# Two-block decoder forward pass: sums and splits at the start, the order of work in both attentions, and the heads and tails of the second block's layers

## The reference, cut to what matters

```python
# first block, two layers; adaptive scale, shift and gate come from silu(c) @ ada_w + ada_b
h  = rmsnorm(x,  norm_mix[i]) * (1.0 + sc1) + sh1
hc = rmsnorm(xc, norm_mix[i]) * (1.0 + csc1) + csh1
y, yc = diff_attention(...)  if i == 0 else neighbourhood_attention(...)   # q, k, v = h @ wqkv; o @ wo
x = x + g1 * y
x = x + g2 * conv_ffn(h2, ...)      # up, 3-tap conv, silu(g) * a, down; h2 = rmsnorm(x) scaled, shifted
# (xc is carried along the same way in layer 0)

# _diff_attend, layer 0: 8 heads, two maps each
p = softmax(s);  a = p[:, :, 0] - lam * p[:, :, 1];  o = rmsnorm(a @ v, subln) * (1.0 - lam_init)
# neighbourhood_attention, layer 1: 16 heads, scores + relative bias under a mask, then softmax @ v

# second block, two layers
h = rmsnorm_2(x, norm_g);  proj = h @ w_in          # nsa, pool, conv, fox, gates, merges
for i, o in enumerate((o_nsa, o_pool, o_conv, o_fox)):
    acc += sigmoid(merge[:, :, i]) * ((o * silu(gates[:, :, i])) @ w_branch[i])
x = x + acc @ w_out
# at the end
return rmsnorm_2(x, final_norm_g)
```

## Time and profile before

| | |
|---|---|
| median of 3 runs | 1707.87 us (1707.37 to 1710.95) |
| profiled execution | 1705.45 us, its span 1703.6 us, mean granted TensorE clock 0.983 |
| busy, share of the span | PE 1623.3 us (95%), PEld (weight loads, beside PE) 1421.4, DVE 874.5, ACT 743.6, POOL 540.6 |
| share of the chain that ended last | PE 87%, DVE 3%, POOL 3%, DMA 3%, issue 2%, ACT 2% |
| DMA | 249.39 MB, mean 146 GB/s |

### The profile page before, as it was taken

The page is one execution under the profiler, slowest core; times in us unless marked ns, Lnnn a source line. Parts: engine busy times, 40 slices in busy tenths (PEclk is TensorE's granted clock), DMA queues, the critical chain, the costliest instruction groups (busy, mean ns, idle before and its releaser), DMA issues.

```text
span 1703.6 us, 26688 instructions
## 1 busy us (share of the span) xinstructions
PE 1623.3 (95%) x10996; PEld 1421.4 (83%) x10996; DVE 874.5 (51%) x1382; ACT 743.6 (44%) x1341; POOL 540.6 (32%) x358
## 2 busy tenths in 40 slices
PE   8999986999999999999979999999999999999997
PEld 6679655868777888868957899999999999999997
DVE  3335375347533554333165688647475445468334
ACT  3323375345422443334256555445544444554342
POOL 1224045223210222220254111115423565433553
PEclk9999999999999999999999999999999999999998
DMA  9154401344246222366232455553535543534551
GB/s 393 51 222 173 177 22 50 102 170 173 84 167 230 79 81 84 118 211 215 94 75 83 145 184 180 155 189 128 194 125 173 174 167 120 198 124 134 185 181 46
DMA packets 52904, 249.39 MB, mean 146 GB/s; under 512 B 20656, under 2 KB 21680, under 8 KB 26288
## 3 DMA queue, kind: packets, MB, share of 16 engines
q1 hardware_dynamic: 44320, 244.42, 41.2%
q10 hardware_dynamic: 8464, 3.28, 0.8%
HBM read 246.63 MB, written 1.05 MB: 145 GB/s over the span
## 4 chain that ended last, share of the span: by engine, by line
PE 87%; DVE 3%; POOL 3%; DMA 3%; issue 2%; ACT 2%; POOLq 0%; DVEq 0%; SPq 0%; ACTq 0%
PE psq L520 19%; PE psq L521 19%; PE psq L522 19%; PE ps L520 6%; PE ps L522 6%; PE ps L521 6%; DMA RAW<-wstream 2%; PE ps L533 2%; PE ps L665 1%; PE psq L1022 1%; PE psq L1905 1%; DVE STAT L1074 1%; PE ps L579 1%; PE ps L1002 0%; DVE WL L502 0%
## 5 line engine op out<-in xcount | busy, mean ns | idle before, releaser
L520 PE MATMUL psq<-NH,WH 128*128 128x256 f32 (+1 forms) x1904 | 600.2, 315 | 13.6 <-POOL NL L2229 5.0
L521 PE MATMUL psq<-NL,WH 128*128 128x256 f32 (+1 forms) x1904 | 592.1, 311 | 0.0
L522 PE MATMUL psq<-NH,WL 128*128 128x256 f32 (+1 forms) x1904 | 592.0, 311 | 0.0
L502 DVE TENSOR_TENSOR WL<-RAW,WH 128x1024 fp32r<-128x1024 f32 (+3 forms) x264 | 322.9, 1247 | 387.2 <-ACT WH L492 387.2
L502 POOL TENSOR_TENSOR WL<-RAW,WH 128x1024 fp32r<-128x1024 f32 (+2 forms) x116 | 292.2, 2521 | 533.7 <-ACT WH L492 533.6
L492 ACT ACTIVATE WH<-RAW 128x1024 fp32r<-128x1024 f32 (+2 forms) x380 | 361.1, 1001 | 194.1 <-DMA RAW<-wstream 151.7
L520 PEld LDWEIGHTS psq<-NH,WH 128*128 128x128 f32 x1904 | 368.6, 194 | 45.9 <-issue 19.6
L522 PEld LDWEIGHTS psq<-NH,WL 128*128 128x128 f32 x1904 | 368.7, 194 | 18.2
L521 PEld LDWEIGHTS psq<-NL,WH 128*128 128x128 f32 x1904 | 369.2, 194 | 17.1
L520 PE MATMUL ps<-NH,WH 128*128 128x256 f32 (+1 forms) x368 | 121.9, 331 | 2.5 <-DVE WL L502 1.9
L521 PE MATMUL ps<-NL,WH 128*128 128x256 f32 (+1 forms) x368 | 121.2, 329 | 0.0
(11 more groups left out here) (326 smaller groups left out, 2543.7 us busy)
## 6 DMA issues: line engine op xcount, KB each, us to landing
RAW<-wstream SPq DMA_DIRECT2D x196, 1024.0 KB, 4.9
RAW<-wstream SPq DMA_DIRECT2D x32, 704.0 KB, 4.1
K<-first SPq DMA_DIRECT2D x4, 1024.0 KB, 13.1
X<-xin SPq DMA_DIRECT2D x2, 1024.0 KB, 6.0
V<-first SPq DMA_DIRECT2D x2, 1024.0 KB, 19.0
Q<-first SPq DMA_DIRECT2D x2, 1024.0 KB, 26.4
BR<-rpb ACTq DMA_DIRECT2D x8, 256.0 KB, 9.5
BR<-rpb SPq DMA_DIRECT2D x8, 256.0 KB, 8.5
```

Of the source, the lines that this page charges most:

```text
L502: e.tensor_tensor(WL[:, u % 3, a:z], RAW[:, v % 3, a:z], WH[:, u % 3, a:z].bitcast(F32), ALU.subtract).then_inc(w_lo_p if pool else w_lo_v, 1)
L520: e.matmul(o, lh, rh, start=start, stop=False)
L521: e.matmul(o, lh, rl, start=False, stop=False)
L522: return e.matmul(o, ll, rh, start=False, stop=stop)
```

## The change

The parts, in the order of the program:

1. Start: the square sums become eight matmuls with a block of ones 32 columns wide, in four strips of PSUM (`pe_strip_sums`), a copy and four one-column products (`pe_strip_join`). The constants are loaded in two parts, `first(0)` before unit 0, `first(1)` before unit 1, and so on. `FIRST_PIECES` is another table, and units 1 and 2 are split at j = 1, 2 instead of 1, 3.
2. Diff attention: `wo` units 0 to 2 are loaded before the `ada` 2 weights and split during the V projections; `ada` 2 runs in steps 2 to 9; DVE takes age 6 first in each step and then goes from young to old; the first four k of `wo` unit 0 run in steps 33 to 36, and head 7's turn stands before k = 6 and not k = 5.
3. Neighbourhood attention: scores of pairs 0 to 3 stand among the last V projection, whose four query tiles are now written one after the other (`pe_last_values`); bias chunk 3 is completed in steps 10 and 11; k = 0 to 5 of `wo` (1, 0) run in steps 17 to 20.
4. `wo` (1, 1) and (1, 2), `up` (1, 0) and `out` units 0 to 2 are multiplied k by k over both output tiles (`pe_tiles`, `pe_halves`), so that each k is wanted later than before; `wo` (1, 3) and `out` unit 3 finish in two products, one per output tile and bank.
5. Second block, both layers: `kc`, `qn`, `kn` are multiplied with x times the norm's gain, not yet divided by the root mean square; their high and low parts (`act_raw_hi`, `dve_raw_lo`) lie in the free half of `NH` and `NL` and are made as the residual tiles come; DVE multiplies by the row 1/rms when it copies the three results out (`dve_raw_out`, in place of ACT's copy). The usual norm runs beside these products. In layer 0, the residual x takes its own norm and gain after `kn`'s turn.
6. Last branch: the split of the next unit's `WL` stands behind the split of the sums.
7. End: the final gain is multiplied in by ACT when each tile is complete, then four DVE products of two tiles each, and four stores.

The diff, cut to its core:

```diff
+    for i in range(3):
+        add(("wo", 0, i), 1, run=False)
     for k in range(DT):
         add_ada(2, k)
         run_ada(2, k)
-    for i in range(4):
-        add(("wo", 0, i), 1000 if i else 1)
+    add(("wo", 0, 3), 1000, run=False)
+    runs += [("wo", 0, i) for i in range(4)]
...
-    on_pool = [[KEYS[v] == ("wo", 0, 0), v in SPLIT_AT and SPLIT_AT[v] % POOL_EVERY[v] == 0] for v in range(NU)]
+    on_pool = [[False, v in SPLIT_AT and SPLIT_AT[v] % POOL_EVERY[v] == 0] for v in range(NU)]
...
-            return SPLIT_AT[UNIT_OF[key]] + (3 if key[:2] == ("qkv", 0) else 2)
+            return SPLIT_AT[UNIT_OF[key]] + (3 if key[:2] in (("qkv", 0), ("wo", 0)) else 2)
...
                 mm = e.matmul(NB[:, width * q:width * q + width], t[:, q * P:q * P + P], GSQ[:, m, :] if n == 5 else ONE,
                               start=first and q == 0, stop=m == DT - 1, skip_group_check=True)
+            mm.then_inc(sq_sum, 1)
+
+        def pe_strip_sums(e):
+
+            e.wait_ge(c_zero, 3)
+            for m in range(DT):
+                wait_square(e, 0, m)
+                s = 32 * (m % 4)
+                mm = e.matmul(NB[s:s + 32, :], ONE32, sq_tile(0, m), start=m < 4, stop=m >= 4)
+            mm.then_inc(strip_mm, 1)
+
+        def dve_strips(e):
+            e.wait_ge(strip_mm, 1)
+            e.tensor_copy(PP[:, 0, :], NB[:, :]).then_inc(strip_sb, 1)
+
+        def pe_strip_join(e):
+            e.wait_ge(strip_sb, 1)
+            e.wait_ge(d_const, 16)
+            for q in range(4):
+                mm = e.matmul(NB[:, q:q + 1], PP[:, 0, q * P:q * P + P], const_at("sel", 0, 1), start=True, stop=True)
             mm.then_inc(sq_sum, 1)
 
...
+        def pe_tiles(e, key, b, js, ks, xh, xl, wait_x):
+
+            v, wh, wl = weights(key)
+            for k in ks:
+                wait_weights(e, v, k)
+                wait_x(k)
+                for j in js:
+                    o = b[:, 256 * j:256 * j + 256]
+                    w = slice(P * j, P * j + P)
+                    e.matmul(o, wh[:, k, w], xh[:, k, 0:256], start=k == 0 and j == 0, stop=False, skip_group_check=True)
+                    e.matmul(o, wh[:, k, w], xl[:, k, 0:256], start=False, stop=False, skip_group_check=True)
+                    mm = e.matmul(o, wl[:, k, w], xh[:, k, 0:256], start=False, stop=k == DT - 1, skip_group_check=True)
+            return mm
+
+        def pe_halves(e, key, b, wait_x):
+            pe_tiles(e, key, b, (0, 1), range(DT), NH, NL, wait_x).then_inc(gemm, 1)
 
...
+                if l == 0 or i < 3:
                     split_hi(e, ahead(key))
...
-            for i in range(3 if l else 1):
+            for i in range(3 if l else 4):
                 split_lo(e, ahead(("qkv", l, 8 + i)), False)
...
-                if n < DT:
-                    pe_ada(e, 2, n)
-                if n == 9:
+                if 2 <= n < DT + 2:
+                    pe_ada(e, 2, n - 2)
+                if n == 11:
                     pe_ada_turn(e, 2)
+                if 33 <= n < 37:
+                    if n == 33:
+                        e.wait_ge(att_exp, 62)
+                    pe_abreast(e, ("wo", 0, 0), [bank[0], bank[1]], (n - 33,), pe_wait_heads)
...
-                if n in (34, 36):
-                    split_hi(e, SPLIT_AT[UNIT_OF["wo", 0, (n - 34) // 2]])
...
-                for age, j in each_step(n, 11, 32)[::-1]:
+                for age, j in sorted(each_step(n, 11, 32), key=lambda x: (x[0] != 6, x[0])):
...
-                if n == 36:
-                    split_lo(e, SPLIT_AT[UNIT_OF["wo", 0, 1]], False)
...
-                if n == 34:
-                    split_lo(e, SPLIT_AT[UNIT_OF["wo", 0, 0]], True)
...
+        def pe_last_values(e):
+
+            key = ("qkv", 1, 11)
+            v, wh, wl = weights(key)
+            for q in range(4):
+                pe_na_qk(e, q)
+                if q == 0:
+                    e.wait_ge(v_sb, 10)
+                o = bank[4 + q // 2][:, 256 * (q % 2):256 * (q % 2) + 256]
+                c = slice(q * P, q * P + P)
+                for k in range(8):
+                    if q == 0:
+                        wait_weights(e, v, k)
+                    mm = mm3(e, o, NH[:, k, c], NL[:, k, c], wh[:, k, :], wl[:, k, :], k == 0, k == 7)
+                if q % 2 == 1:
+                    mm.then_inc(gemm, 1)
...
+                if 4 <= p < 16:
+                    pe_na_qk(e, p)
+                if n in NA_FILL:
+                    if n == 17:
+                        e.wait_ge(att_exp, EXP1 + 30)
+                    pe_tiles(e, ("wo", 1, 0), bank[0], (0, 1), NA_FILL[n], NH, NL, lambda k: pe_wait_pairs(e, k))
+
+        NA_FILL = {17: (0, 1), 18: (2, 3), 19: (4,), 20: (5,)}
...
-                if n in (4, 5, 8, 9):
-                    pool_bias(e, 2 if n < 8 else 3, n % 4)
+                if n in (4, 5, 10, 11):
+                    pool_bias(e, 2 if n < 8 else 3, n % 2)
...
                 else:
-                    pe_wide(e, ("wo", l, i), [bank[i][:, 0:256], bank[i][:, 256:512]], 256, NH, NL, wait_x)
+                    if i == 0:
+                        pe_tiles(e, ("wo", 1, 1), bank[1], (0, 1), range(6), NH, NL, wait_x)
+                        pe_tiles(e, ("wo", 1, 0), bank[0], (0, 1), (6, 7), NH, NL, wait_x).then_inc(gemm, 1)
+                    elif i == 1:
+                        pe_tiles(e, ("wo", 1, 1), bank[1], (0, 1), (6, 7), NH, NL, nothing).then_inc(gemm, 1)
+                    elif i == 2:
+                        pe_halves(e, ("wo", 1, 2), bank[2], nothing)
+                    else:
+                        pe_wide(e, ("wo", 1, 3), [bank[3][:, 0:256], bank[4][:, 0:256]], 256, NH, NL, nothing)
...
+                    if l == 1 and m:
+                        dve_raw_lo(e, 0, m - 1)
+                if l == 1:
+                    dve_raw_lo(e, 0, DT - 1)
 
...
+        def act_raw_hi(e, l, m):
+            e.wait_ge(x_res, x_ready(5 + l, m))
+            if l == 0 and m == 0:
+                e.wait_ge(g_pair, 4)
+            e.activation(XH[:, m, :], X[:, m, 0:256], ACT.Copy, scale=norm_gain(5 + l, m, 0)).then_inc(raw_hi, 1)
+
+        def dve_raw_lo(e, l, m):
+            e.wait_ge(raw_hi, 8 * l + m + 1)
+            e.scalar_tensor_tensor(out=XL[:, m, :], in0=X[:, m, 0:256], scalar=norm_gain(5 + l, m, 0),
+                                   in1=XH[:, m, :].bitcast(F32), op0=ALU.mult, op1=ALU.subtract).then_inc(raw_lo, 1)
+
...
+        def dve_last(e):
+            e.wait_ge(rs_bc, NORM_AT[7] + 1)
+            for a in range(4):
+                x = X[:, 2 * a:2 * a + 2, 0:256]
+                e.wait_ge(x_gain, 2 * a + 2)
...
+        def pe_raw_head(e, l):
+            n = 5 + l
+            wait_x = lambda k: e.wait_ge(raw_lo, 8 * l + k + 1)
+            tiles = lambda name, js, ks: pe_tiles(e, unit_key(l, name), ring_bank(name), js, ks, XH, XL, wait_x)
+            e.wait_ge(x_res, x_ready(n, 5))
+            tiles("kc", (0, 1), range(6))
+            if l:
+                pe_sums(e, n, 6)
+            pe_sums(e, n, 7)
+            tiles("kc", (0, 1), (6, 7)).then_inc(gemm, 1)
+            e.wait_ge(x_res, x_ready(n, 7))
+            tiles("qn", (0,), range(DT))
+            pe_rs_rows(e, n)
+            tiles("qn", (1,), range(DT)).then_inc(gemm, 1)
...
+        RS_ROW = TMP[:, 5, 0:256]
+
+        def dve_raw_out(e, l, name):
+            at = RAW_UNITS.index(name)
+            dst = (KC[:, :, :], wide2(TMP[:, 6, :]), wide2(TMP[:, 8, :]))[at]
+            rs = RS_ROW.unsqueeze(1).to_broadcast([P, 2, 256])
+            e.wait_ge(raw_rs, l + 1)
+            e.wait_ge(gemm, product(unit_key(l, name)))
+            e.scalar_tensor_tensor(out=dst, in0=pair(ring_bank(name)), scalar=0.125 if name == "qn" else 1.0, in1=rs,
+                                   op0=ALU.mult, op1=ALU.mult).then_inc(raw_copy, 1)
...
         def dve_branch(e, l, n):
-            split_lo(e, ahead(branch_key(l, n)), False)
+            if n < 3:
+                split_lo(e, ahead(branch_key(l, n)), False)
...
         def pool_branch(e, l, n):
-            split_lo(e, ahead(branch_key(l, n)), True)
+            if n < 3:
...
                     split_sum_lo(e, l, mp)
+                split_lo(e, ahead(branch_key(l, n)), True)
 
 
         def pe_out(e, l):
...
-                pe_wide(e, ("out", l, i), [b[:, 0:256], b[:, 256:512]], 256, NH, NL, wait_x if i == 0 else nothing)
+                if i < 3:
+                    pe_halves(e, ("out", l, i), b, wait_x if i == 0 else nothing)
+                else:
+                    pe_wide(e, ("out", l, i), [b[:, 0:256], bank[2][:, 0:256]], 256, NH, NL, nothing)
...
-        FIRST_PIECES = (([], []), ([], [(0, 0)]), ([(0, 1)], [(1, 0), (1, 1)]), ([(0, 2)], [(1, 2)]),
-                        ([(0, 3)], [(1, 3), (2, 0), (2, 1)]), ([(2, 2)], [(0, 4), (1, 4), (2, 3)]),
-                        ([(2, 4)], [(0, 5), (1, 5), (2, 5)]), ([(0, 6)], [(1, 6), (2, 6), (0, 7), (1, 7), (2, 7)]))
```

(10 more changed lines are left out.)

287 lines of the change are left out of this document (195 added, 92 removed).

## The result

The changed kernel takes 1681.89 us, median of four runs (1680.89 to 1682.3), against 1708.59 of before beside it: a ratio of 0.9837, with a 95% interval from 0.9822 to 0.9851. That is 26.7 us faster, where 57 were forecast; it lies above the range.

A forecast was written before the change was run, and what follows sets the result against it. PE, busy 95% of the span, was taken to bound the kernel; idle gaps, low clock and needless start sums could go. Terms summed to -56.5 us: 1648.9 for the profiled execution, 1651 for the median, range 1642 to 1662.

The forecast's parts named there:

- Step 7: Second block's two heads: shorter stretch from norm sums to kn's end, -7.1 and -7.0 us (each -4 to -8.5).
- Step 3: Diff attention's steps: age 6 first removes PE's six waits for DVE's copy-out, -5.5 us (0 to -6).
- Step 8: out of both layers: sums ready earlier with POOL's and DVE's splits behind them, -4.8 and -4.0 us (each -2.5 to -5.5).
- Step 6: wo (1, 3) and up (1, 0): finishing tile by tile and k-outer order shorten five waits, -2 us (0 to -3).
- the start: Kernel start: strip sums replace 64 one-column matmuls, pe_first(0) begins at 13.9, -5 us (-3 to -7).
- neighbourhood attention with its entry: Neighbourhood attention: waits at entry (-2.7), for the bias transfer (-6.3) and at the tail (-2) shrink, -11 us (-7 to -13).
- the end: Kernel end: four DVE products and four stores instead of eight, -1.6 us (-0.5 to -2.5).
- the entry: Diff attention's entry: splits ahead of the first maximum delay exponentials and third scores, +1.5 us (0 to +4).
- The tail: Diff attention's tail: earlier splits and wo products in the steps remove idle time and low clock, -10 us (-7 to -11).
- rival (c): Products in pe_tiles order: costlier matmuls make the kernel slower, 1765 at 0.15 us each; chance 2 in 100.
- The gap at the third scores: Diff attention's entry: a PE gap over 3 us at the third scores would show the forecast wrong.
- Rival (a): Whole kernel: about half the gain, several places falling short, -27 us or 1681; chance 2 in 10.

The follow-up runs named there:

- the kernel with both splits first: Changed kernel with kn's copy, then DVE's low-part splits of qf's and kf's weights ahead of turns, compress inputs among the forget logs, layer 0's residual gain late: 1672.92 us.
- the last kernel: Against the kernel with all three edits: forget logs' first DVE instructions ahead of both turns, vf's split and the compress inputs behind the logs: 1667.04 us.
- the kernel with all three edits: Changed kernel with both splits first in the heads, age 3's scalar first in diff attention, POOL's split held behind DVE's low parts at out: 1661.33 us.

## Why the prediction was wrong

**Step 7, the heads, failed: -14.1 forecast, +7.6 measured.** Its first half held: 19.8 us to `vn` where 18.5 was worked out, against 25.6. What failed is the half sentence "the three copies change from ACT to DVE", priced at nothing. ACT stood idle at that place (3.27 us ahead of its copy); DVE had the compress inputs, two turns and three splits there, some of them stretched by POOL (4.97 us for the four instructions of L1843, which took 2.38 in the kernel before). What stands behind a moved step on its new queue, and ahead of it, was not listed. That the loss lies in the heads is shown by the old heads (-6.2 in span), and that it is the order of that queue by the kernel with both splits first (17.0 us again, with DVE's work stretched as much as in the changed kernel). The one such wait of up to 2.5 us that was named, on the last low parts, did not come.

**Step 3, the steps: -5.5 forecast, +0.1 us per head measured (11.05 instead of 10.96).** The bound at zero was the right value: "another wait of the step takes over". The waits for POOL's mix grew from 0.95 to 1.47 and those for its norm from 0.20 to 0.48, because the scalar for POOL came later. The reason given for slack (another step of the head) was wrong: DVE's queue joins the steps. With the scalar first the steps give 6.1 us.

**Step 8, `out`: -8.8 forecast, -2.9 measured.** The stretching of L2248 was read rightly, and moving POOL's split removed it there (its first took 0.69 instead of 2.18). But the split went from beside one DVE instruction with two SBUF inputs to beside another, the low parts. The rule was at hand and was weighed only for the heads. With the split held back as well, the two stages gave 9.4.

**Step 6: -2 forecast, 0 measured.** PE waits 1.90, 1.04 and 1.80 us around that norm instead of 0.68, 1.03 and 1.81. No experiment was made on it, so the cause of the missing 2 us stays open.

**Right:** the start (-4.5; `pe_first(0)` begins at 12.96, not 13.9, and PE then waits 3.01 at its selection), neighbourhood attention with its entry (-14.7, against -11), the end (-1.5). Of the 14.7, some are luck: 1.1 is a shorter wait for a transfer on the way, and the stretch to its first transposes, 524.97 us here, took 525.99 to 528.50 in the twelve kernels of the experiments, which have the same code there. In diff attention the entry costs what was said: the third scores wait 3.32 us, at a clock of 0.75 in the 10 us from 190, and the first turn comes 36.14 us behind the first scores instead of 34.24. The tail gives about 10: from the end of the heads' last step to the norm's sums it is 42.0 us instead of 52.5.

Of the signs named ahead, the wait L1002 on DVE in the steps is gone, no wait of `kc` for low parts came, and the spacing inside `pe_tiles` is 0.12 us, so that rival (c) is out. Between 275 and 300 us two gaps above 1 us are left (1.64 and 1.07). The gap at the third scores, named as a sign of being wrong, came. No sign was named for a bank that is freed late.

Rival (a), half of the gain at -27 with "no gain in 3" and 0.2 of chance, is what came, to 0.3 us, but with other parts: it had -8 for the heads, which gave +7.6, and -7 for neighbourhood attention, which gave -14.7. That its total fits is luck.

## What to carry to other kernels

Before a copy-out or a split changes engines, write down all that stands ahead of it on the new queue at that moment, and what PE can't start without it: its bank, its weights, the next. Here the wait moved to the next item in the queue until the whole order was right; in the two heads together, the orders in between gave +1.0, -2.2 and -3.6 us against the changed kernel, and the whole order -10.2. And when a POOL instruction is moved, look at which DVE instruction with two SBUF inputs it lands beside.

## What the runs showed of the hardware

- The price of a gap was not set by its length alone. In the last kernel, behind a gap of 3.14 us, the granted clock was 0.50, the lower of the two levels (1.2 GHz), from 1164 to 1180 us, though PE was busy for 6.17 of the first 6.20 us and for all of the next 10; these were the compress products and the start of the next ones. In the kernel with all three edits, the gap of 3.30 us ahead of `vf` was followed by 0.81 in the 10 us from 1150 and 0.85 in the next, and the whole head is 5.7 us shorter.
- The same code behind the same gap got different clocks in different executions. At the entry of diff attention PE waits 3.3 us for the third scores in all thirteen kernels with the change, whose code there differs at most in DVE's order within a step. From the first scores to the first turn it then took 33.31 us in two of them, at a granted 1.00 in the 16 us from the first scores, 34.81 to 35.41 in three at 0.89, and 35.90 to 36.23 in eight at 0.79. A later stretch with transfers under way (DMA busy for 0.45 of it) but no wait of PE for them took 131.5 us in all fourteen kernels, the one before included, to 0.02. So an effect of 2 us is read between two instructions with no such gap and no wait for a transfer between them.
- Even an instruction with one tensor in SBUF was held. In the last kernel `TENSOR_SCALAR` on 128x8 began at 1144.05 and ended at 1146.38, as POOL's split of 1143.96 to 1146.36 ended; it took 2.33 us in the other layer too, again beside such a split (1417.43 to 1419.83). The same instruction takes 0.17 in the changed kernel.
